# Memory heads before the index steps, softmax from PSUM, and another order at the end, in a one-core decoder step

## The reference

```python
u, cB, cC, q, k, v, qi, ki, wi, qm, g = split_proj(x, pos, w_in, b_gate)   # one input projection
conv_out = short_conv(u, cB, cC)                                           # branch A
attn_out = sparse_attn(q, k, v, qi, ki, wi)                                # branch B: 8 heads x 64, an indexer picks the keys
mem_out  = softmax(qm @ mk.T * 64 ** -0.5) @ mv                            # branch C: 4 heads x 64, 256 memory tokens
m = sigmoid(g0) * (conv_out @ w_br_conv) + sigmoid(g1) * (attn_out @ w_br_attn) + sigmoid(g2) * (mem_out @ w_br_mem)
h = layernorm(alpha * x + m @ w_o)
y = layernorm(alpha * h + hier_moe(h))         # 4 groups of 8 experts, 1024 -> 2 x 256 -> 1024, two per token
```

## Time and profile before

| | |
|---|---|
| PE busy | 535.9 us, 89% of the span |
| DVE, ACT, POOL busy | 279.9, 104.7, 63.8 us |
| TensorE's granted clock, mean | 0.959 |
| DMA | 163.53 MB, 272 GB/s over the span |
| gate tiles, L796 | 384 matmuls, 94.2 us |
| a gate activation, L1434 | 24, 478 ns each, from PSUM 128x264 |
| a copy of 512 columns from PSUM, L1391 | 16, 597 ns each |
| chain that ended last | PE 55%, DMA 19%, DVE 17%, ACT's queue 5% |

### The profile page before, as it was taken

The page is one execution under the profiler, slowest core; times in us unless marked ns, Lnnn a source line. Parts: engine busy times, 40 slices in busy tenths (PEclk is TensorE's granted clock), DMA queues, the critical chain, the costliest instruction groups (busy, mean ns, idle before and its releaser), DMA issues.

```text
span 601.3 us, 8683 instructions
## 1 busy us (share of the span) xinstructions
PE 535.9 (89%) x3518; PEld 327.6 (54%) x3518; DVE 279.9 (47%) x767; ACT 104.7 (17%) x246; POOL 63.8 (11%) x70
## 2 busy tenths in 40 slices
PE   8999999999999995999899998969999993985770
PEld 4556566565688773777676557524655351521220
DVE  1363766667677687779862597302101100101026
ACT  1001111011310124455200231111111010101021
POOL 0000000001200024488300000000000000000002
PEclk9999999999999996999999999979999998898886
DMA  8981241944443446566989947799999999999951
GB/s 293 399 311 53 87 141 43 375 147 143 140 125 123 141 132 200 177 227 194 328 332 409 334 153 311 267 422 382 422 414 419 421 421 419 422 419 419 417 228 72
DMA packets 47918, 163.53 MB, mean 272 GB/s; under 512 B 5986, under 2 KB 22844, under 8 KB 35844
## 3 DMA queue, kind: packets, MB, share of 16 engines
q1 hardware_dynamic: 39312, 139.81, 60.8%
q0 software_dynamic: 3472, 14.31, 7.1%
q10 hardware_dynamic: 5092, 8.83, 4.2%
HBM read 160.14 MB, written 2.77 MB: 271 GB/s over the span
## 4 chain that ended last, share of the span: by engine, by line
PE 55%; DMA 19%; DVE 17%; ACTq 5%; issue 2%; ACT 1%; SPq 0%; POOLq 0%; POOL 0%; DVEq 0%
PE bank L796 12%; PE bank L605 11%; DMA ring<-in_w_down 10%; PE bank L1159 6%; DMA ring<-in_w_up 5%; PE bank L553 4%; PE bank L1251 3%; ACTq L1516 2%; PE bank L651 2%; DMA proj<-in_w_down 2%; ACTq L1515 2%; PE bank L619 2%; PE bank L1134 2%; PE bank L1116 2%; PE bank L1194 2%
## 5 line engine op out<-in xcount | busy, mean ns | idle before, releaser
L796 PE MATMUL bank<-work,ring 128*128 128x264 f32 x384 | 94.2, 396 | 0.0
L605 PE MATMUL bank<-ring,work 128*128 128x512 f32 (+2 forms) x224 | 91.1, 544 | 0.4 <-DVE work L1746 0.4
L796 PEld LDWEIGHTS bank<-work,ring 128*128 128x128 f32 x384 | 71.2, 192 | 14.8 <-issue 2.8
L1159 PE MATMUL bank<-ring,work 128*32 128x512 f32 x304 | 50.7, 653 | 14.5 <-DMA ring<-in_w_up 11.2
L605 PEld LDWEIGHTS bank<-ring,work 128*128 128x128 f32 x224 | 39.8, 190 | 30.4 <-issue 26.6
L2399 DVE SCALAR_TENSOR_TENSOR work<-work,bank 128x256 f32<-128x256 f32 x8 | 3.4, 422 | 87.5 <-ACT work L1576 87.5
L2411 DVE COPY gates<-bank 128x512 f32<-128x512 f32 x8 | 5.5, 692 | 81.9 <-PE bank L1251 73.2
L1159 PE MATMUL bank<-proj,work 128*32 128x512 f32 x128 | 28.9, 593 | 6.0 <-DMA ring<-in_w_up 3.7
L1251 PE MATMUL bank<-ring,work 128*32 128x512 f32 x176 | 29.6, 664 | 4.5 <-DMA ring<-in_w_down 3.8
L1159 PEld LDWEIGHTS bank<-ring,work 128*32 128x32 f32 x304 | 13.5, 119 | 36.3 <-issue 36.2
L922 PE MATMUL bank<-work,ring 128*128 128x264 f32 x128 | 31.8, 392 | 0.4 <-DVE gates L2137 0.3
(11 more groups left out here) (340 smaller groups left out, 834.7 us busy)
## 6 DMA issues: line engine op xcount, KB each, us to landing
ring<-in_w_up SPq DMA_DIRECT2D x19, 2048.0 KB, 20.1
ring<-in_w_down SPq DMA_DIRECT2D x13, 2048.0 KB, 25.6
ring<-in_w_in SPq DMA_DIRECT2D x21, 1024.0 KB
proj<-in_w_up SPq DMA_DIRECT2D x7, 2048.0 KB, 22.5
misc<-in_w_up SPq DMA_DIRECT2D x5, 1024.0 KB, 25.8
gates<-in_w_up SPq DMA_DIRECT2D x5, 1024.0 KB, 21.1
ring<-in_w_o SPq DMA_DIRECT2D x4, 1024.0 KB, 11.0
proj<-in_w_down SPq DMA_DIRECT2D x2, 2048.0 KB, 24.3
```

Source lines behind the costliest of these rows:

```text
L605: last = mm(bank[2 * (i % 2) + t][:, 0:w], lhs[:, k, 128 * t:128 * t + 128], rhs[:, k % 4, :], start=(k == 0), stop=(k == KT - 1))
L796: last = mm(b[:, 0:TOK], w[:, k, 128 * (n % 2):128 * (n % 2) + 128], xT[:, k, 0:TOK], start=(k == 0), stop=(k == KT - 1))
L1159: last = mm(bank[5][32 * j:32 * j + 32, :], xTe[q // 2 % 2][:, k, s0:s0 + CAP], up_of(n + j // 2, j % 2, r), start=(k == 0), stop=(k == KT ...
```

## The change

- `PAIR_TILES` begins at pair 2. Pairs 0 and 1 leave the loops and are written out between the compaction and the index steps on PE, ACT and DVE.
- For memory heads the factor 0.125 goes into the copy of the turned queries. DVE's pass into `P1` goes, the maximum is taken in PSUM (`mem_max`), both key tiles in one instruction, and the exponential reads PSUM.
- All top-k rounds left after the index steps run before pair 2. Key sums and key dots move one pair later; the last pair has six sums.
- On PE, half tiles split the compaction's exchanges; tiles 14 to 17 stand around pair 1's values and before pair 2, and ACT takes their four activations before the exponentials of heads 4 and 5.
- At the end the last load is two loads of 512 columns. `down_last` puts two filler products and the combining products between the halves; the second norm's order changes, and the second half of tile 1 is scaled by DVE rather than ACT.

```diff
-PAIR_TILES = ((15, 16), (17, 18), (19, 20), (21, 22), (23, None), (None, None))
+MEM_PAIRS = NMH // 2
+PAIR_TILES = {2: (18, 19), 3: (20, 21), 4: (22, 23), 5: (None, None)}
-KEY_SUMS = ((), (), range(0, 3), range(3, 6), range(6, 9), range(9, 12))
-KEY_DOTS = ((), range(12, 13), range(13, 15), range(15, 17), (), ())
+KEY_SUMS = ((), (), (), range(0, 3), range(3, 6), range(6, 12))
+KEY_DOTS = ((), (), range(12, 13), range(13, 15), range(15, 17), ())
...
         def score_bank(n):
-            return bank[2 + n] if n < 2 else bank[n % 2]
+            return bank[2 + n % 2] if n < NMH else bank[n % 2]
...
@@ last_down
+                if f == 0:
+                    sp.dma_start(d, s[:, :, f, :]).then_inc(quad_in[w], 16)
+                else:
+                    sp.dma_start(d[:, :, 0:512], s[:, :, f, 0:512]).then_inc(quad_in[w], 16)
+                    sp.dma_start(d[:, :, 512:1024], s[:, :, f, 512:1024]).then_inc(tail_in, 16)
...
@@ PE
+            pe.wait_ge(comp_in, 1)
+            mm(bank[7][:, 152:153], c("below"), scan[:, 128:129], start=True, stop=True)
+            mm(bank[7][:, 153:154], c("block"), small[:, 12:13], start=True, stop=True).then_inc(comp_ps, 1)
+            scores(0)
+            gate_tile(8, k1=4)
+            pe.wait_ge(comp_in, 2)
...
+            gate_tile(8, k0=4)
+            gate_tile(9, k1=2)
+            pe.wait_ge(comp_in, 3)
...
+            gate_tile(9, k0=2)
+            gate_tile(10)
+            turn(0)
+            turn(1)
+            index_scores(0)
+            gate_tile(11)
+            pe.wait_ge(comp_in, 4)
...
+            values(0)
+            scores(1)
+            index_scores(2)
+            gate_tile(12)
+            index_scores(4)
+            gate_tile(13)
+            turn(2)
+            turn(3)
+            gate_tile(14)
+            values(1)
+            scores(2)
+            for n in range(15, 18):
+                gate_tile(n)
...
+            def down_last():
...
+                unit_there(n)
+                products(0, 0)
+                products(0, 1).then_inc(used_w, 1)
+                for _ in range(2):
+                    mm(bank[5][:, :], ident, h3[:, 0, 0:512], start=True, stop=True)
+                unit_there(n + 1)
+                products(1, 0).then_inc(y_half, 1)
+                pe.wait_ge(y_act, QUADS)
+                combine_end(0, 0)
+                pe.wait_ge(tail_in, 16)
+                products(1, 1).then_inc(used_w, 1)
+                combine_end(1, 0)
+                pe.wait_ge(y_dve, QUADS)
+                combine_samples(q)
+                combine_end(0, 1)
+                combine_end(1, 1)
...
@@ ACT
-                    last = act.activation(dst, b[:, lo:hi], ACT.Copy)
+                    last = act.activation(dst, b[:, lo:hi], ACT.Copy, scale=0.125 if n in QM_JOBS else 1.0)
...
-                    act.activation(s, s, ACT.Exp, bias=stats[:, st + t:st + t + 1],
+                    act.activation(s, score_bank(n)[:, at:at + w] if n < NMH else s, ACT.Exp, bias=stats[:, st + t:st + t + 1],
...
+            exps(0)
+            gate_out(8)
+            exps(1)
+            normalise(0)
+            normalise(1)
+            gate_out(9)
+            gate_out(10)
+            act.wait_ge(o_conv, 48)
+            turned_probs(0)
+            turned_probs(1)
+            index_relu(0)
+            index_relu(1)
+            gate_out(11)
             index_relu(2)
             index_relu(3)
-            exps(0)
+            gate_out(12)
+            exps(2)
             index_relu(4)
-            exps(1)
-            normalise(0)
+            exps(3)
             gate_out(13)
+            normalise(2)
             index_relu(5)
-            normalise(1)
...
+            normalise(3)
+            turned_probs(2)
+            turned_probs(3)
+            for n in range(14, 18):
+                gate_out(n)
+            exps(4)
+            exps(5)
+            normalise(4)
+            normalise(5)
+            for p in range(MEM_PAIRS, PAIRS_H):
+                turned_probs(2 * p)
+                turned_probs(2 * p + 1)
...
@@ DVE
+            def mem_max(n):
+                dve.wait_ge(at_s, n + 1)
+                if n >= 2:
+                    dve.wait_ge(at_t, n - 1)
+                st = stats[:, 8 * (n % 2):8 * (n % 2) + 8]
+                link(V.tensor_reduce(st[:, 0:2], score_bank(n)[:, :].rearrange("p (t n) -> p t n", t=2), AX.X, ALU.max,
+                                     negate=True), at_m)
...
+                if i == 1:
+                    head_out(0)
                 if i == 2:
-                    softmax(0)
+                    mem_max(2)
                 if i == 3:
-                    softmax(1)
+                    mem_max(3)
                 if i == 4:
-                    inverse(0)
+                    inverse(2)
                 if i == 5:
-                    inverse(1)
-            for p in range(PAIRS_H):
-                r0, r1, r2 = TOPK_ROUNDS[p]
-                for i in range(r0, r1):
-                    topk_round(i)
+                    inverse(3)
+            for i in range(INDEX_ROUNDS[-1][1], 2 * TOPP // 8):
+                topk_round(i)
+            head_out(1)
+            softmax(4)
+            softmax(5)
+            inverse(4)
+            inverse(5)
+            for p in range(MEM_PAIRS, PAIRS_H):
...
@@ DVE, the end
             y_sums(0, 0)
             y_sums(1, 0)
+            dve.wait_ge(more_c, 1)
+            link(V.bn_stats(stats[:, 24:30], bank[4][:, 0:256]))
...
             y_centre(0, 0)
-            y_rstd(0, 4)
             y_rstd(1, 5)
             y_shift(1, stats[:, 46:47], stats[:, 54:55], n1_ready)
...
+            y_rstd(0, 4)
+            y_scale(0, 0, y_ready)
             y_rstd(2, 6)
-            y_shift(2, mean_s, stats[:, 55:56], ns_ready)
-            y1b, cs1 = y3[:, 1, 512:1024], slice(512, 1024)
-            dve.wait_ge(n1_done, 2)
-            tt(y1b, y1b, ln2g[:, cs1], ALU.mult)
-            tt(y1b, y1b, ln2b[:, cs1], ALU.add, y1b_ready)
+            y_shift(2, mean_s, stats[:, 55:56], n1_ready)
+            y_centre(0, 1)
+            y_scale(0, 1, y_ready)
+            y_centre(1, 1)
+            y_scale(1, 1, y1b_ready)
```

More of the change, by code:

```diff
@@ L781, in gate_hook, with gate_tile @@
                 hooks[0] += 1
-            def gate_tile(n, then=None, part=None):
+            def gate_tile(n, then=None, k0=0, k1=KT):
                 b = bank[gate_bank(n)]
-                if part == 1:
+                if k0:
                     pass
@@ L792, in gate_tile @@
                 w = slot(unit_slot(u)).rearrange("p (k n) -> p k n", k=KT)
-                if n % 2 == 0 and part != 1:
+                if n % 2 == 0 and k0 == 0:
                     pe.wait_ge(unit_sem(u), UC[u])
-                for k in range(4 * (part == 1), 4 if part == 0 else KT):
+                for k in range(k0, k1):
                     last = mm(b[:, 0:TOK], w[:, k, 128 * (n % 2):128 * (n % 2) + 128], xT[:, k, 0:TOK],
@@ L858, in scores @@
                             last.then_inc(at_s, 1)
-            gate_tile(10)
-            index_scores(0)
-            gate_tile(11)
-            pe.wait_ge(comp_in, 4)
-            for g in range(NPG):
-                for j in range(4):
-                    last = mm(bank[7][32 * j:32 * j + 32, 384:416], Alo4[:, j, g, :],
-                              Ahi4[:, j, g, :], start=(g == 0), stop=(g == NPG - 1))
-            last.then_inc(comp_ps, 1)
-            gate_tile(12)
-            index_scores(2)
-            scores(0)
-            gate_tile(13, part=0)
-            index_scores(4)
-            gate_tile(13, part=1)
             def turn(n):
@@ L903, in values @@
                             last.then_inc(at_v, 1)
-            gate_tile(14, part=0)
+            pe.wait_ge(comp_in, 1)
[4 more added lines that the diff above has]
+            pe.wait_ge(comp_in, 2)
+            mm(bank[7][:, 156:157], c("below"), scan[:, 128:129], start=True, stop=True)
+            mm(bank[7][:, 157:159], c("block"), small[:, 13:15], start=True, stop=True).then_inc(comp_ps, 1)
+            gate_tile(8, k0=4)
+            gate_tile(9, k1=2)
+            pe.wait_ge(comp_in, 3)
+            tr(bank[7][:, 0:128], eq[:, 0:128])
+            tr(bank[7][:, 256:384], gt[:, 0:128]).then_inc(comp_ps, 1)
+            gate_tile(9, k0=2)
[5 more added lines that the diff above has]
+            pe.wait_ge(comp_in, 4)
+            for g in range(NPG):
+                for j in range(4):
+                    last = mm(bank[7][32 * j:32 * j + 32, 384:416], Alo4[:, j, g, :],
+                              Ahi4[:, j, g, :], start=(g == 0), stop=(g == NPG - 1))
+            last.then_inc(comp_ps, 1)
+            values(0)
[11 more added lines that the diff above has]
+                gate_tile(n)
             def branch_tile(j):
@@ L931, in _ @@
                 ahead, behind = PAIR_TILES[p]
-                if p == 0:
-                    gate_tile(14, part=1)
```

(6 more changed lines are left out.)

126 lines of the change are left out of this document (48 added, 78 removed).

## The result

The changed kernel takes 611.77 us (median of four, 610.49 to 612.58), the kernel before 603.51 (median of four): ratio 1.0155, 95% interval 1.0123 to 1.0187. (The quotient of these two medians is 1.0137; the ratios here are the recorded ones, with their intervals.) It is slower, by 8.3 us between the medians, and the 607.4 forecast is 4.4 too low. The ratios leave out the few executions in the chip's slower state, one each of e2 (609.25 us) and e6 (916.83 us) among them. The profiled execution took 610.49 us, its span 608.7 (before 601.3), its mean granted clock 0.951 (before 0.959).

What follows compares the result with a forecast made beforehand. PE was taken to bound the run to 310 us, then transfers, with the weight stream starting when the samples' value products end. 603.22 + 6.2 (late sample maximum) - 3.0 (end) = 606.4, plus 1.0 to the median: 607.4 us, range 601.5 to 610.5.

Steps and rivals of the forecast that it cites:

- Compaction: Before the index steps: pair 0's scores and turns on PE make the row numbers come 1.5 us late.
- Index steps: Heads 2 and 3 come ready when heads 0 and 1 did; PE's waits stay, 4.7 and 2.2 us.
- Rival A: Waits before the turns of heads 2 and 3 and the slow clock go: 597 us, chance 0.08.
- Tiles 14 to 17: ACT's order leaves PE 3.3 us idle before head 4's turn, which still comes 1.6 us earlier, at 259.2.
- Branch tile 0: Start of the branch tiles on PE: one more tile before it and an exposed activation make it 3.1 us later.
- Tile 23's activation: Right before branch tile 0: PE waits 0.7 us for it, which the values of pair 4 hid before.
- Key sums: Before the sample maximum: six late sums on DVE and POOL's late products put it and the stream 6.2 us later.
- Product buffers: POOL's four: product 7 waits for the fourth sum, making the sample maximum 6.3 us later, against 5.3 by DVE alone.
- The end: Last down projection and second norm: variances 1.7 us earlier, the whole end 3.0 us shorter.
- the two fillers: Between the halves of the last down projection: they keep PE busy and take 0.9 us together.
- Rival F: Both halves of the last load land together, so the tail gives only 1.8 us: 608.6 us, chance 0.07.
- case E: PE falls to half speed behind a wait at 256 or 294, 1.6 us each: 609 to 610.6 us, chance 0.13.

Runs made afterwards that it cites:

- e2: The kernel before with only the change's end (last_down, down_last, second norm): ratio 0.9994.
- e6: The changed kernel with POOL multiplying key tiles in place, so that no product waits for a sum: ratio 1.0131.
- e4: The changed kernel with ACT taking heads 4 and 5 before the activation of gate tile 17: ratio 1.0069.
- e5: The changed kernel with filler products in PE's two new waits, three before head 4's turn and five before the sample maximum's: ratio 1.0078.
- e3: The changed kernel with key sums one pair earlier, three each in pairs 2 to 5 as before: ratio 1.0051.
- e9: The changed kernel with the edits of e3 and e4, and without the end's two filler products: ratio 0.9975.
- e7: The kernel before with the change's end, without its two filler products: ratio 0.9929.
- e1: The kernel before with only the change's head part, all edits up to the branch tiles: ratio 1.0117.
- e8: The changed kernel with e3's sums, tiles 14 and 15 in PE's waits, ACT reordered, key products in place between key gathers, value gathers in one run: ratio 1.0177.
- e11: e10 plus the change's maximum and exponential from PSUM, heads not moved, and products in place, four to a pair: ratio 0.9873, 594.63 us.
- e12: e8 with the 16 value gathers issued four to a pair instead of in one run: ratio 1.0008.
- e10: The kernel before with tile 14, half of tile 15 and pair 1's scores in PE's waits, tile 13's activation earlier, and e7's end: ratio 0.9901.

## Why the prediction was wrong, step by step

1. *Compaction: right.* The row numbers end at 219.06 against 216.32, 1.5 later once the drift is off; forecast 1.5.
2. *Index steps: right.* Forecast: the pair is gained and the waits stay, 4.7 and 2.2. Trace: 4.52 and 1.61. The exponential from PSUM takes 0.47 (0.5 taken). Rival A is out. (The half speed that the prediction reads from 231.7 on begins at 231.3 by the trace, where the window from 231 to 232 has 0.65; no term uses it.)
3. *Tiles 14 to 17: mechanism right.* Wait 3.3 forecast, 3.01 measured; turn 0.7 earlier than forecast; e4 shows that ACT's order alone makes the wait. The step that failed first is here: it put nothing into the sum for the slow clock behind the wait, 1.0 by e5.
4. *Branch tile 0: +3.1 forecast, +3.5 measured*; those two terms (-0.7, +1.1 by the rows) are the difference. Tile 23's activation: 0.7 forecast, 0.57 measured.
5. *Key sums: right in kind, too small.* The maximum's turn is 7.1 later, not 6.2: 0.4 from step 4, the rest from DVE and POOL. Again the sum holds nothing for the clock behind the wait: it cost 1.35 us more, of which e5 gives back 1.3. So the stream's start is +8.45, not +6.2. e3 takes 4.6 of it back (2.1 of this by its clock before the branch tiles), e4 3.5 (drifts off); e9, which has both edits, 7.3. Product buffers, the cause I named, are a bound only 0.7 above DVE's own (e6).
6. *The end: the step that failed most.* I counted the two fillers 0.9 us; they took 1.98, and as no wait was left for them to cover, all of it lay on the path. The variances, forecast 1.7 earlier after the last turn (572.74 to 588.1 before), came 0.95 later (581.19 to 597.5), and 1.1 earlier without the fillers (e7, 571.87 to 586.1). So the fillers' price is 1.1 of the 2.65 missed there. The rest is missing from e7 too: combining products of 1.12 where 0.9 was taken, the last two 1.98 for 1.7, and 1.0 at the statistics, because DVE takes the samples' three short operations (0.43, 0.18, 0.22) between them. Behind the variances the new order gave 2.0 (1.3 forecast). That e7's end is 3.1 shorter, nearly the forecast's 3.0, is luck: the forecast had reached its figure with fillers on the path and with other terms. Rival F, that the halves land together, is out: the products ran on without a wait.

From the span forecast of +3.2 to the +7.4 of the trace: drift 1.2, branch tile 0.4, sums 0.5, clock behind the maximum 1.35, less 1.2 absorbed in the expert stage, the end 1.95. That is 4.2. Two steps of the sum failed: the clock, put at nothing, and the fillers, put at half their price and into a wait that was not there. Both mistakes are of the same kind, since the rows at hand had the price. I treated the clock as a rival with a chance of 0.13 (case E, 609 to 610.6), although show the same thing after a wait of 2.10, and the same trace has 4.97 followed by 0.57. It was likelier than not and belonged in the sum. And I took the fillers, products of 512 columns, at 0.45 us each (0.9 for two), where each takes 0.99. In float32 a product is two records, and one of 128x128 by 512 columns takes 0.5; the same sum has 0.9 for one combining product of this very shape. Had both been in, the forecast would have been 607.4 + 2.4 + 1.1 = 610.9, against 611.77; the terms still wrong then (drift, what the expert stage absorbed, the rest of the end) partly cancel.

## What to carry to other kernels

A wait on PE costs its length and then, in most of the cases here, what the slow clock takes behind it; put both in the sum from rows of the same trace, the second with a chance of its own. Before you insert work to bridge a wait, look for the wait in a trace without that work: here it was absent, and the bridge was the loss. When stages are reordered, check each engine's own order against who waits for it: undoing one activation ahead of two heads' exponentials gave back 0.9%, and moving the key sums one pair forward (three instead of six in the last pair) 1.0%, though the two together gave less than their sum.

## What the runs showed that I had not expected

- *The length of a wait does not settle what the clock does behind it.* Waits of 3.01 in the changed kernel, e1 and e6, of 3.24 in e6, of 2.95 in e8 and e11 and of 2.09 in e12 were followed by a granted clock of 0.5; the wait of 2.10 in the earlier trace rows was too. The same 3.01 in e3, 3.14 in e10 and 2.19 in e9 were followed by 1.00. The waits of 3.78 and more were all followed by 0.5, unless fillers stood in them (e5).
- *Gathers in a run stop other engines.* In e8, 16 value gathers 1.25 us apart, with the DMA share near 0.7, go with halts of 0.2 to 2.0 us of PE between matmuls of one tile, for which the profile names no semaphore, and with 13.88 us of idle DVE. In e12 runs of eight, four and four leave 0.4 us. The view of the DMA queues has one block of instructions (16 KB) there: in e8 between 271 and 272, and the gate tile with the halts starts at 272.57; in e12 between 268 and 269, and the halts follow at 269.27. Such a block lands in the kernel before (270 to 271) and in the changed one (271 to 272) too, where POOL's gathers alternate with products, and there PE has no halt: the block alone does not make one. The row for each stretch of 1 us (packets, MB, share of 16 engines), e8, then e12:

```profile
q8 instruction: 1, 0.02, 7.0%
```

```profile
q8 instruction: 1, 0.02, 6.0%
```

  From there PE's loads of its stationary operand in e8 start 0.7 or 1.4 us apart (273.99, 274.70, 276.10, 276.81, 278.23), as if instructions came one at a time. That fits engines that wait for their instructions while the gathers' descriptors are served. Which of the two is held up by what is argued, not shown.
- *DVE is free of POOL when POOL only issues gathers.* The key dot's multiplication takes 2.0 when it starts beside a POOL product (2.00 at 278.53 in the changed kernel) and 0.69 at 268.02, where POOL waits for a sum, and 0.69 throughout e12's pairs, where POOL issues gathers and multiplies nothing. The prediction expected this of pair 2.
- *Executions differ by 2.6 us before any changed line.* The first comparison row stands between 196.96 and 199.59 in the profiled executions, so places in two traces are compared only with it taken off. In the two latest, e8 and e9, 1.7 and 1.45 of it are the clock: four products of 512 columns near 148 take 3.68 and 3.43 instead of 1.98, at a granted clock of 0.5, with PE busy 15.8 of the 16 us from 136 to 152. A slow stretch can come without a wait.
